# The down projection of a two-block model on one Trainium2 core: weight sums made by accumulating transfers instead of on VectorE, three buffers instead of five, and another order of products

## The reference

```python
h2 = rms_norm(x, norm_mlp[l])
x = x + jnp.square(jax.nn.relu(h2 @ w_up[l])) @ w_down[l]     # w_up 1024x4096, w_down 4096x1024
return rms_norm(x, norm_final)
```

## The kernel before

| due | VectorE, before | VectorE, after |
|---|---|---|
| 46.2 | eviction of P2, s=0 | eviction of P7, s=0 |
| 48.2 | eviction of P2, s=1 | eviction of P7, s=1 |
| 49.8 | output of row block 2 (L2001) | the same |
| 51.8 | output of row block 3 | the same |
| 52.2 | eviction of P4, s=0 | the same |
| 54.2 | output of row block 0 | the same |
| 56.2 | eviction of P4, s=1 | the same |
| 60.2 | output of row block 1 | the same |

## Time and profile before

### The profile page before, as it was taken

How to read it: one execution, slowest core, us unless ns; L and a number is a source line. 1 busy time by engine, 2 the same in 40 slices (tenths; PEclk the granted TensorE clock), 3 DMA queues, 4 the chain that set the end, 5 groups by cost and what they waited for, 6 DMA issues and landing times.

```text
span 1079.8 us, 14177 instructions
## 1 busy us (share of the span) xinstructions
PE 1071.6 (99%) x5092; PEld 858.6 (80%) x5092; DVE 764.1 (71%) x1296; ACT 547.1 (51%) x930; POOL 158.6 (15%) x257
## 2 busy tenths in 40 slices
PE   9999999999999999999999999999999999999997
PEld 7787787887777788767778888888888888888886
DVE  7888887867889854455556645555896796796795
ACT  6766766565666544244344423335453443453455
POOL 2000000120755321022133400021000000000003
PEclk9999999999999999999999999999999999999999
DMA  6422232332120233311323223224503503503301
GB/s 234 142 68 101 79 98 88 118 117 89 44 95 23 76 108 106 98 59 59 107 88 99 78 79 98 86 90 140 192 1 116 215 1 113 200 1 107 146 1 79
DMA packets 30486, 103.65 MB, mean 96 GB/s; under 512 B 3408, under 2 KB 4304, under 8 KB 30416
## 3 DMA queue, kind: packets, MB, share of 16 engines
q1 hardware_dynamic: 29984, 101.89, 27.9%
q10 hardware_dynamic: 432, 0.86, 0.2%
HBM read 100.11 MB, written 2.10 MB: 95 GB/s over the span
## 4 chain that ended last, share of the span: by engine, by line
PE 97%; DVE 1%; ACT 1%; DMA 0%; issue 0%; DVEq 0%; ACTq 0%
PE ps L951 25%; PE ps L953 24%; PE ps L952 24%; PE ps L914 5%; PE ps L913 5%; PE ps L912 5%; PE ps L1062 3%; PE ps L1090 2%; PE ps L1123 2%; PE ps L1117 1%; PE ps L862 1%; DMA raw<-wst 0%; PE ps L989 0%; PE ps L1023 0%; DVE xtok L2001 0%
## 5 line engine op out<-in xcount | busy, mean ns | idle before, releaser
L951 PE MATMUL ps<-xgh,wh 128*128 128x512 f32 x847 | 335.4, 396 | 0.5 <-DVE wl L1494 0.3
L953 PE MATMUL ps<-xgh,wl 128*128 128x512 f32 x847 | 330.2, 390 | 0.0
L952 PE MATMUL ps<-xgl,wh 128*128 128x512 f32 x847 | 329.9, 389 | 0.0
L1494 DVE TENSOR_TENSOR wl<-raw,wh 128x1024 fp32r<-128x1024 f32 x146 | 183.8, 1259 | 50.4 <-ACT wh L1162 49.3
L1162 ACT ACTIVATE wh<-raw 128x1024 fp32r<-128x1024 f32 x146 | 153.0, 1050 | 84.6 <-PE ps L953 64.6
L951 PEld LDWEIGHTS ps<-xgh,wh 128*128 128x128 f32 x847 | 159.0, 188 | 38.7 <-issue 7.0
L953 PEld LDWEIGHTS ps<-xgh,wl 128*128 128x128 f32 x847 | 159.0, 188 | 33.7
L952 PEld LDWEIGHTS ps<-xgl,wh 128*128 128x128 f32 x847 | 159.2, 188 | 32.0 <-issue 0.2
L1373 ACT ACTIVATE Pt<-Pt,stat 128x256 f32<-128x256 f32 (+2 forms) x128 | 64.3, 503 | 99.3 <-DVE stat L1770 40.2
L912 PE MATMUL ps<-wh,fh 128*128 128x512 f32 x224 | 87.1, 389 | 0.0
L913 PE MATMUL ps<-wl,fh 128*128 128x512 f32 x224 | 87.1, 389 | 0.0
(11 more groups left out here) (243 smaller groups left out, 1710.5 us busy)
## 6 DMA issues: line engine op xcount, KB each, us to landing
raw<-wst SPq DMA_DIRECT2D x146, 512.0 KB, 3.4
b<-wdn SPq DMA_DIRECT2D x32, 512.0 KB, 6.9
bst<-nbias SPq DMA_DIRECT2D x8, 256.0 KB, 3.4
gx<-xT SPq DMA_DIRECT2D x3, 512.0 KB, 6.6
outT<-xtok SPq DMA_DIRECT2D x3, 512.0 KB, 2.6
masks<-msk SPq DMA_DIRECT2D x2, 256.0 KB, 3.7
sq<-fin SPq DMA_DIRECT2D x2, 256.0 KB, 4.3
cstt<-cst SPq DMA_DIRECT2D x1, 448.0 KB, 5.5
```

Source lines behind the costliest of these rows:

```text
L951: e.matmul(o, high, a, start=(k == 0), stop=False)
L952: e.matmul(o, high, b, start=False, stop=False)
L953: done = e.matmul(o, low, a, start=False, stop=stop)
L1494: e.tensor_tensor(wl_t[:, v % NHL, :], src, f32(wh_t[:, v % NHL, :]), ALU.subtract).then_inc(lo_done, 1)
```

## The change

- The products come in the order P1, P5, P2, P6, P3, P7, P4 (before: P1, P5, P6, P3, P7, P2, P4). P6, P7 and P4 follow on the same banks 0 and 1; P7 is now directly followed by P4.
- `weight_sums_here` is gone. GpSimd issues, eight times a round, a transfer that adds a quarter from HBM to a buffer in SBUF (`accum_op=ALU.add`). A transfer can only add, so all sums are sums without minus, and the signs go into the sums of activations (two of them become `scalar_tensor_tensor` with -1) and into the evictions (four of the seven products are subtracted from `xtok`).
- Buffers: `bw` takes B11, B21, B22 one after the other (P1, P2, P3), each plain loaded when the one before is split. `bt` is loaded with B11, and gets B12 (then P5 is split), B22 (P6) and B21 (P4) added. `bu` is loaded with B22 and gets B12 added (P7). A transfer that overwrites or adds to a buffer waits for the split that read it (`unit_split`). A round has 10 plain loads on SP and 8 accumulating transfers on GpSimd, of 512 KB each.
- The late offset of the split of P5's second unit (3.2) is gone. `row_tick` follows the new order; `row_norms`, `row_outs` and `row_done` stay as they are.

```diff
-PARTS = ("P1", "P1", "P5", "P5", "P6", "P6", "P3", "P3", "P7", "P7", "P2", "P2", "P4", "P4")
+PARTS = ("P1", "P1", "P5", "P5", "P2", "P2", "P6", "P6", "P3", "P3", "P7", "P7", "P4", "P4")
...
-            n = 2 * r + kk + 1
-            if p in ("P1", "P2", "P3"):
...
+            b, landed, n = {"P1": (bw, bw_in, 3 * r + 1), "P2": (bw, bw_in, 3 * r + 2), "P3": (bw, bw_in, 3 * r + 3),
+                            "P5": (bt, bt_sum, 3 * r + 1), "P6": (bt, bt_sum, 3 * r + 2), "P4": (bt, bt_sum, 3 * r + 3),
+                            "P7": (bu, bu_sum, r + 1)}[p]
+            q.wait_ge(landed[kk], 16 * n)
...
-                late = {("P5", 1): 3.2, ("P4", 1): -1.5}.get(ch.units[u][0][2:], 0.0)
+                late = {("P4", 1): -1.5}.get(ch.units[u][0][2:], 0.0)
...
-            return ev_at["dn", FINAL, "P2" if n > 1 else "P4", n % 2] + 1.0
+            return ev_at["dn", FINAL, "P7" if n > 1 else "P4", n % 2] + 1.0
...
+            def down_plain():
+                for r in range(ROUNDS):
+                    for kk in range(2):
+                        yield UNIT_AT[form_no[r - 1, "P3", kk]] + 3.0 if r else UP_AT[0] + 6.0 + 5.0 * kk
...
+                        e.dma_start(bw[:, kk, :], wdn[8 * r + DN["11", kk], :, :]).then_inc(bw_in[kk], 16)
+                    for freed, quarter in (("P1", "21"), ("P2", "22")):
+                        for kk in range(2):
+                            yield UNIT_AT[form_no[r, freed, kk]] + 3.0
+                            unit_split(q, form_no[r, freed, kk])
+                            e.dma_start(bw[:, kk, :], wdn[8 * r + DN[quarter, kk], :, :]).then_inc(bw_in[kk], 16)
...
-            def weight_sums_here():
...
-                e.tensor_tensor(fs[:, 0, :], a21, a22, ALU.add).then_inc(fs_done, 1)
+                e.tensor_tensor(fs[:, 0, :], a22, a21, ALU.subtract).then_inc(fs_done, 1)
...
-                e.tensor_tensor(fs[:, 2, :], fs[:, 0, :], a11, ALU.subtract).then_inc(fs_done, 1)
+                e.scalar_tensor_tensor(fs[:, 2, :], fs[:, 0, :], -1.0, a11, ALU.mult, ALU.subtract).then_inc(fs_done, 1)
...
-                e.tensor_tensor(x_, bank[ch.bank[name]], x_, ALU.add).then_inc(ev_done, 1)
+                if ADDS_TO[p][1] == "2":
+                    e.tensor_tensor(x_, x_, bank[ch.bank[name]], ALU.subtract).then_inc(ev_done, 1)
+                else:
+                    e.tensor_tensor(x_, bank[ch.bank[name]], x_, ALU.add).then_inc(ev_done, 1)
...
+            def down_sums():
+                for r in range(ROUNDS):
+                    for kk in range(2):
+                        yield UP_AT[r] + 24.0 + 5.0 * kk
+                        q.wait_ge(bt_in[kk], 16 * (r + 1))
+                        e.dma_start(bt[:, kk, :], wdn[8 * r + DN["12", kk], :, :], accum_op=ALU.add).then_inc(bt_sum[kk], 16)
+                    for kk in range(2):
+                        yield UP_AT[r] + 44.0 + 5.0 * kk
+                        q.wait_ge(bu_in[kk], 16 * (r + 1))
+                        e.dma_start(bu[:, kk, :], wdn[8 * r + DN["12", kk], :, :], accum_op=ALU.add).then_inc(bu_sum[kk], 16)
+                    for n, (split, quarter) in enumerate((("P5", "22"), ("P6", "21"))):
+                        for kk in range(2):
+                            yield UNIT_AT[form_no[r, split, kk]] + 3.0
+                            unit_split(q, form_no[r, split, kk])
+                            q.wait_ge(bt_sum[kk], 16 * (3 * r + 1 + n))
+                            e.dma_start(bt[:, kk, :], wdn[8 * r + DN[quarter, kk], :, :], accum_op=ALU.add).then_inc(bt_sum[kk], 16)
```

More of the change, by code:

```diff
@@ L313, in build @@
         sb("gap", [128, 80], F, xs_)
-        b21, t14 = (sb(n, [128, 2, 1024], F, xs_) for n in ("b21", "t14"))
+        bu = sb("bu", [128, 2, 1024], F, xs_)
         xs_.close()
@@ L392, in build @@
         xtok = sb("xtok", [128, 4, D], F, ph)
-        b11, b12, b22 = (sb(n, [128, 2, 1024], F, ph) for n in ("b11", "b12", "b22"))
+        bw, bt, _ = (sb(n, [128, 2, 1024], F, ph) for n in ("bw", "bt", "spare"))
         fa = sb("fa", [128, 2, 4, 256], F, ph)
@@ L405, in build @@
         out_done = sem("out_done")
-        b_in = {q: [sem(f"b{q}_in{i}") for i in range(2)] for q in (11, 12, 21, 22)}
+        bw_in, bt_in, bu_in = ([sem(f"{n}_in{i}") for i in range(2)] for n in ("bw", "bt", "bu"))
+        bt_sum, bu_sum = ([sem(f"{n}_sum{i}") for i in range(2)] for n in ("bt", "bu"))
         fin_in, piece_done = sem("fin_in"), sem("piece_done")
@@ new lines, in down_plain @@
+                    for freed, quarter in (("P1", "21"), ("P2", "22")):
[6 more added lines that the diff above has]
+                    for kk in range(2):
+                        yield UNIT_AT[form_no[r - 1, "P4", kk]] + 3.0 if r else UP_AT[0] + 16.0 + 5.0 * kk
+                        if r:
+                            unit_split(q, form_no[r - 1, "P4", kk])
+                        else:
+                            q.wait_ge(tile_done, C_END)
+                        e.dma_start(bt[:, kk, :], wdn[8 * r + DN["11", kk], :, :]).then_inc(bt_in[kk], 16)
@@ new lines, in down_thirds @@
+            def down_thirds():
+                for r in range(ROUNDS):
+                    for kk in range(2):
+                        yield UNIT_AT[form_no[r - 1, "P7", kk]] + 3.0 if r else UP_AT[0] + 30.0 + 5.0 * kk
+                        if r:
+                            unit_split(q, form_no[r - 1, "P7", kk])
+                        else:
+                            x_turned(q)
+                        e.dma_start(bu[:, kk, :], wdn[8 * r + DN["22", kk], :, :]).then_inc(bu_in[kk], 16)
@@ L836, in stores @@
                 q.wait_ge(out_done, 16 * 5)
-            merge([weights(), starts(), attention_masks(), biases(), swaps(), downs(), gains(), stores()])
+            merge([weights(), starts(), attention_masks(), biases(), swaps(), down_plain(), down_sums(), down_thirds(), gains(), stores()])
         @block.tensor
@@ L2109, in row_gains, with down_sums @@
                     e.tensor_scalar(x_, x_, stat[:, 3, 4 + n:5 + n], 1.0, ALU.mult, ALU.mult).then_inc(out_pool, 1)
-            lanes = [zeros(), first_sums(), row_gains()] + [sums(s) for s in (1, 2, 3)]
+            def down_sums():
+                for r in range(ROUNDS):
+                    for kk in range(2):
+                        yield UP_AT[r] + 24.0 + 5.0 * kk
+                        q.wait_ge(bt_in[kk], 16 * (r + 1))
+                        e.dma_start(bt[:, kk, :], wdn[8 * r + DN["12", kk], :, :], accum_op=ALU.add).then_inc(bt_sum[kk], 16)
+                    for kk in range(2):
+                        yield UP_AT[r] + 44.0 + 5.0 * kk
+                        q.wait_ge(bu_in[kk], 16 * (r + 1))
+                        e.dma_start(bu[:, kk, :], wdn[8 * r + DN["12", kk], :, :], accum_op=ALU.add).then_inc(bu_sum[kk], 16)
+                    for n, (split, quarter) in enumerate((("P5", "22"), ("P6", "21"))):
+                        for kk in range(2):
+                            yield UNIT_AT[form_no[r, split, kk]] + 3.0
+                            unit_split(q, form_no[r, split, kk])
+                            q.wait_ge(bt_sum[kk], 16 * (3 * r + 1 + n))
+                            e.dma_start(bt[:, kk, :], wdn[8 * r + DN[quarter, kk], :, :], accum_op=ALU.add).then_inc(bt_sum[kk], 16)
+            lanes = [zeros(), first_sums(), row_gains(), down_sums()] + [sums(s) for s in (1, 2, 3)]
             lanes += [head_low(i) for i in range(LOW_BY_VECTOR, SPLIT)]
```

22 lines of the change are left out of this document (5 added, 17 removed).

## The result

| | before | after |
|---|---|---|
| time, median of 13 runs (lowest to highest) | 1081.61 us (1081.45 to 1081.96) | 1083.97 us (1083.85 to 1084.48) |
| span of the profiled execution | 1079.8 us | 1082.1 us |
| PE / DVE / POOL busy | 1071.6 / 764.1 / 158.6 us | 1072.0 / 729.2 / 186.1 us |

A forecast was written before the change was run, and what follows sets the result against it. TensorE's gapless matmuls were taken to bound the kernel. Span 1079.8 + 0.7 (bank wait) + 2.3 (last norm) = 1082.8 us, with 1.8 around it 1084.6 us; forecast's own range 1083.7 to 1086.0, 8 in 10 range 1082.0 to 1087.5.

The forecast's parts named there:

- What bounds the kernel: Feed-forward stage: TensorE's matmuls run without a gap, 0.2267 us each; work taken off VectorE is worth 0.
- `scalar_tensor_tensor`: The two sums of activations: at most some 0.05 us more for each of 32, beside matmuls, so cost 0.
- Accumulating transfers: GpSimd's adding transfers: landing taken as 7 us, between 3.4 and a far end of 28; cost 0 at 7 us.
- the tight sum: Down phase, B22 added for P6's second unit: the sum with least time, 11.7 us before TensorE stands.
- The rival in which each of VectorE's instructions holds a transfer's start: Within late sums (0.14): holds of at most 1.22 us, one or two fitting in the room of 11.7 - 7.
- The estimate of 3.2 or 4.4 us: GpSimd's transfer: 2.0 us plus bytes by 436 GB/s, 3.2 us for 512 KB or 4.4 for both streams.
- The room of 11.7 us: P6's second sum: time its transfer may take before TensorE stands; beyond it, cost 4 x (X - 11.7).
- Bank wait: P7 directly before P4, rounds 0 to 2: P4's s=1 comes 0.24 us late, cost 3 x 0.24 = 0.7 us.
- The last norm: Kernel's end: ScalarE's halves delay rows and outputs, P4's evictions queue behind outputs on VectorE; cost 2.3 us, 2.0 to 3.0.
- the end stays as it is: Rival at the last norm: evictions start when banks are ready, only the bank wait remains, 1082.3 us; chance 0.19.
- The rival of late sums: Accumulating transfers over 11.7 us make TensorE stand every round; at 14 us 9 us, so 1094 us; chance 0.14.
- Outside the span: Time around the profiled span: 1.8 us unchanged; first use of GpSimd's transfer queue taken as 0, with -0.3 to +1.

The follow-up runs named there:

- the sums alone: The changed kernel with the order of products of before, sums still by accumulating transfers: 1081.55 us, 1.0001 of the time before.
- the two delayed runs: The changed kernel with the issue of P6's second sum held back until 12 or 20 down tiles of the round are done: 1086.49 and 1108.55 us.
- the order alone: The kernel before with only the new order of products and due time of rows, weight sums still on VectorE: 1083.86 us, 1.0022.

## Why the prediction came out right, point by point

- **Time.** 1084.6 predicted, 1083.97 measured; 3.0 us of loss against 2.4. Both terms are there, and both were too large, so the time lies near the lower end of the forecast's range, 1083.7 to 1086.0.
- **What bounds the kernel.** Right. TensorE's matmuls wait for nothing in the stage before or after (the three late weight loads aside), and 35 us less on VectorE moved nothing (1081.55 with the sums alone). The page shows 35 and not 39 us less, as instructions of VectorE overlap: the one behind a split of 1.22 us starts 1.13 us after it, and 32 x 1.13 are about 36.
- **`scalar_tensor_tensor`.** Bounded at 0.05 us each, measured 0: 418 and 425 ns, and 418 and 425 ns as `tensor_tensor`.
- **Accumulating transfers.** 7 us taken, between 3.4 and 28. In the down phases measured 5.2 to 5.6 for the first two of a round, beside little else, and 7.6 to 12.7 for the next two, which have more room; 13.3 at most in the ups phase, where no split waits for them. The choice of the row for loads in company was near; the far end was far too far. The 7 us were a middle value, not a mechanism: what sets the landing is the company, and the tight sum happened to have little of it. The rival in which each of VectorE's instructions holds a transfer's start didn't show: 28 of GpSimd's 32 issues took 0.86 to 0.89 us, the longest 1.24. The estimate of 3.2 or 4.4 us from the Trainium skill (DMA: Bandwidth & Descriptors, "Anatomy of one DMA") was too low for both kinds here: 3.7 plain, 5.4 adding.
- **The room of 11.7 us.** Right, shown by the two delayed runs: landing plus 2.4 us gives 892.0 and 903.4, and TensorE goes on at 892.17 and 903.49. But the room was counted against a landing alone; a sum that is issued later also falls into SP's loads and lands later.
- **Bank wait.** The mechanism, its place and its count are as predicted: P4 s=1, rounds 0 to 2, behind the split. The weight loads are 0.18 us late where 0.24 was worked out; they follow the eviction's end by 0.06 us and not by 0.11 as in the earlier trace rows. The size in time is not as predicted: the step "s=1 comes 0.24 us late. Cost 3 x 0.24" took the lateness of a weight load for TensorE's. TensorE lost 0.27 us in all, about 0.09 each, so the term of 0.7 is 0.27.
- **The last norm.** 2.3 predicted, 2.08 measured. The mis-sized step is the row of 1.36 us, read where each row is followed by a wait's handover; from row 2 to row 3 in one go are 1.18 us (1070.35 to 1071.53), and these 0.18 us are most of the difference. Output 3 follows its row by 1.30 us, forecast 1.32. What the two orders do to each other is shown by altering either.
- **The rival "the end stays as it is"** stands refuted: in the changed kernel the evictions wait behind outputs. The rival of late sums didn't come; its price of 1 us per microsecond of lateness held for stands of up to 3.2 us, and behind the stands of 4.7 us and more the clock added some 2 us each.
- **Outside the span.** Taken as 1.8 us with up to 1 for GpSimd's queue. In the profiled execution it is 1.84 (1083.94 less 1082.1), and 1.84 too in the run with the order alone, which has no transfer from that queue at all. So its first use costs nothing measurable.

## What to carry to other kernels

Where engines run a fixed order, ask of a reordering not only whether each piece still has time, but what stands in front of the last pieces in each queue: an instruction that waits for another engine, one place ahead of an eviction, passes its delay on, here 2.1 us to the end through two such outputs, and moving each of them by one place gave that back. Work taken from an engine that nobody waits for is worth nothing, here 35 us of it. A transfer that adds is a free way to make weight sums as long as its landing, counted in the company that it will have, and the split behind it are over before TensorE comes to the unit.

## What the runs showed of the hardware beyond that

- An accumulating transfer of 512 KB from HBM to SBUF beside little else lands 5.2 to 5.6 us after its issue from GpSimd, a plain one 3.6 to 3.8; GpSimd is held for 0.87 and 0.53 us, and the transfer engines for nearly twice the time by the adding one.
- VectorE's output with two inputs in SBUF took 1.78 us instead of 0.75 beside GpSimd's product of two SBUF tiles that had started 0.06 us ahead of it. Where an output started first (changed kernel, 1071.65 against 1071.72), it kept its 0.75 us and GpSimd's scaling took 1.25 instead of 0.69.
- A weight load 0.18 us late cost TensorE 0.07 us at once and 0.08 to 0.11 us over the phase.
- After TensorE had stood for 5.25 us, its granted clock was 0.50 (1.2 GHz) from 903.4 to 907.4 us, with 0.43 us from matmul to matmul, and 1.00 (2.4 GHz) after that. Behind stands of 4.72 and 5.36 us it was 0.50 too, behind stands of 3.24 and 0.45 us it stayed at 1.00.
